# First mixer: its convolution begins during the projections, its channel norm is summed part by part, and the first loads stand in the order of their use

## The reference, cut to what matters

```
u = x @ conv_w_in                                  # 1024 -> 768 (a) + 768 (gate) + 256 (q_mem)
h = a * sigmoid(gate)
h = depthwise_conv(h, dw_w, 31 taps) + dw_b        # each channel by itself, over the tokens, causal
h = layer_norm(h, ln_g, ln_b)                      # over the 768 channels of a token
y_mix = silu(h)
y_mem = softmax(q_mem k_mem^T / 8) v_mem           # 4 heads, 256 memory rows
x = layer_norm(sqrt(2) * x + concat(y_mix, y_mem) @ w_o, ln1_g, ln1_b)
```

## Time and profile before

| | |
|---|---|
| median of 3 runs | 2316.89 us (2315.36 to 2318.26) |
| the profiled execution: its own time | 2313.38 us |
| its span in the trace | 2311.6 us |
| busy: PE, DVE, ACT, POOL | 2117.9, 1109.6, 757.2, 62.6 us |
| weights read | 597.22 MB, 259 GB/s over the span |
| the first mixer | the first 188 us of the span, about |

### The profile page before, as it was taken

One profiled execution on the slowest core, in us unless ns is written; L12 is line 12 of the kernel. 1 busy time (PEld: TensorE's weight loads), 2 busy tenths in 40 slices (PEclk: granted clock), 3 DMA queues, 4 the chain that ended last, 5 costly groups with the idle time before them and its releaser, 6 DMA issues.

```text
span 2311.6 us, 30755 instructions
## 1 busy us (share of the span) xinstructions
PE 2117.9 (92%) x13056; PEld 1530.9 (66%) x13056; DVE 1109.6 (48%) x1866; ACT 757.2 (33%) x1387; POOL 62.6 (3%) x96
## 2 busy tenths in 40 slices
PE   7968999999979899999898789999999889999998
PEld 7855434433458644344343778999998778999996
DVE  5664232222256632222222566666554466666554
ACT  4743111101135411011110545543443454543442
POOL 3000000000000000000000000010000000020000
PEclk9989999999999899999999899999999899999999
DMA  9307999999974489999999423454545514454552
GB/s 315 115 37 282 427 427 428 427 428 427 425 299 177 157 368 427 427 428 427 428 428 400 157 73 125 142 198 147 180 176 178 182 46 142 153 194 155 183 182 74
DMA packets 129054, 600.32 MB, mean 260 GB/s; under 512 B 5980, under 2 KB 24544, under 8 KB 102672
## 3 DMA queue, kind: packets, MB, share of 16 engines
q1 hardware_dynamic: 124336, 589.32, 64.4%
q10 hardware_dynamic: 3344, 7.79, 0.9%
q0 software_dynamic: 1232, 1.19, 0.3%
HBM read 597.22 MB, written 1.05 MB: 259 GB/s over the span
## 4 chain that ended last, share of the span: by engine, by line
PE 71%; DMA 16%; DVE 8%; ACT 3%; issue 1%; SPq 0%; DVEq 0%; ACTq 0%
PE ps L1458 13%; PE ps L440 10%; PE ps L441 9%; PE ps L442 9%; DMA ring<-in_w_up 8%; DMA rx<-in_w_up 8%; PE ps L1498 6%; PE ps L456 2%; PE ps L458 2%; PE ps L457 2%; DVE ARm L980 2%; PE ps L539 2%; PE ps L2835 2%; PE ps L2837 2%; PE ps L2836 2%; PE ps L1387 1%
## 5 line engine op out<-in xcount | busy, mean ns | idle before, releaser
L416 DVE TENSOR_TENSOR CL<-ring,CH 128x1024 fp32r<-128x1024 f32 x284 | 333.5, 1213 | 248.2 <-ACT CH L411 247.7
L440 PE MATMUL ps<-XTH,CH 128*128 128x256 f32 x1456 | 422.3, 290 | 14.2 <-DVE CL L416 14.2
L441 PE MATMUL ps<-XTL,CH 128*128 128x256 f32 x1456 | 416.1, 286 | 0.0
L442 PE MATMUL ps<-XTH,CL 128*128 128x256 f32 x1456 | 416.0, 286 | 0.0
L1458 PE MATMUL ps<-ring,ARM 128*64 128x512 f32 x1024 | 353.9, 611 | 30.4 <-DMA ring<-in_w_up 20.4
L1458 PE MATMUL ps<-rx,ARM 128*64 128x512 f32 x1024 | 353.7, 608 | 20.8 <-DMA rx<-in_w_up 12.7
L411 ACT ACTIVATE CH<-ring 128x1024 fp32r<-128x1024 f32 x284 | 283.2, 1044 | 122.4 <-PE ps L2837 60.7
L440 PEld LDWEIGHTS ps<-XTH,CH 128*128 128x128 f32 x1456 | 283.7, 195 | 18.2 <-DVE CL L416 15.3
L441 PEld LDWEIGHTS ps<-XTL,CH 128*128 128x128 f32 x1456 | 283.8, 195 | 0.4
L442 PEld LDWEIGHTS ps<-XTH,CL 128*128 128x128 f32 x1456 | 283.5, 195 | 0.0
L1458 PEld LDWEIGHTS ps<-ring,ARM 128*64 128x64 f32 x1024 | 114.8, 141 | 186.3 <-issue 137.6
(11 more groups left out here) (421 smaller groups left out, 3697.5 us busy)
## 6 DMA issues: line engine op xcount, KB each, us to landing
rx<-in_w_gate SPq DMA_DIRECT2D x32, 2048.0 KB, 23.6
ring<-in_w_gate SPq DMA_DIRECT2D x32, 2048.0 KB, 24.9
ring<-in_w_down SPq DMA_DIRECT2D x32, 2048.0 KB, 27.2
ring<-in_w_ffn SPq DMA_DIRECT2D x30, 2048.0 KB, 8.2
ring<-in_w_up SPq DMA_DIRECT2D x28, 2048.0 KB, 27.0
rx<-in_w_down SPq DMA_DIRECT2D x28, 2048.0 KB, 27.2
rx<-in_w_up SPq DMA_DIRECT2D x28, 2048.0 KB, 27.3
ring<-in_w_in SPq DMA_DIRECT2D x14, 2048.0 KB, 8.6
```

The source lines that it names most:

```text
L416: v.e.tensor_tensor(pc.lo[:, cs], pc.ap[:, cs], pc.hi[:, cs].bitcast(F), ALU.subtract).then_inc(dve_done, v.put("lo", pc.k, q))
L440: p.e.matmul(o, pc.hi[:, c, n0:n0 + 128], src[0][:, c, :], start=c == 0, stop=False)
L441: p.e.matmul(o, pc.hi[:, c, n0:n0 + 128], src[1][:, c, :], start=False, stop=False)
L442: m = p.e.matmul(o, pc.lo[:, c, n0:n0 + 128], src[0][:, c, :], start=False, stop=c == nk - 1)
```

## The change

1. Loads. `mem` comes in two halves; `x` moves from ACT's queue into SP's, behind `w_mem_kv`; the norm's gain and bias (`load_gb`) are issued behind the projections; 20 small loads for the router and later stages (`g_route_loads`) leave the start of POOL's queue and wait for projection u0. The weights of the convolution are loaded and cut so that pieces come in the order memory queries, a and gate of blocks 0 and 1, of 2 and 3, of 4 and 5.
2. Projections in the order `U_ORDER`, with the memory scores, exp and normalization among them. DVE multiplies `a` straight out of PSUM (no copies `CA`), and runs 20 taps between the splits.
3. Taps: 80 on TensorE (18 of j = 3, all of j = 4 and 5, block after block), 106 on DVE, those of two or three blocks in turn, most with `own(1)` in place of `own()`.
4. Norm: a first mean `M0` over blocks 0 and 1 is subtracted from each block as it gets ready; its sum and its squares are added up block by block (`SUMS`), and the variance is the mean square less the square of the mean. The end is done for each half of the tokens apart, and ACT applies SiLU twice, once for the product itself and once for its high half.
5. Output tiles: chunks 6 and 7 (the memory part) of the first four tiles are done first and left open in PSUM. `dve_router` moves behind tile (1, 1), its sums behind (2, 1).

```diff
@@ sp_all, loads
-            y.e.dma_start(MEM, I["mem"][0].rearrange("(t p) d -> p t d", p=128)).then_inc(mem_in, 16)
...
+        def y_first_loads(k):
+            if k == 0:
+                for t in range(2):
+                    y.e.dma_start(MEM[:, t, :], I["mem"][0, 128 * t:128 * t + 128, :]).then_inc(mem_in[t], 16)
+            if k == 1:
+                y.e.dma_start(X, I["x"][0].rearrange("(t p) d -> p t d", p=128)).then_inc(x_in, 16)
...
+        def g_route_loads():
+            g.wait_ge(pe_done, p.at("u", 0))
@@ taps
-        ON_PE = 9
-        taps = [(k, j) for k in range(31) for j in ((3, 4, 5, 2) if k < ON_PE else (3, 4, 5))]
+        U_ORDER = (12, 13, 0, 1, 6, 7, 2, 3, 8, 9, 4, 5, 10, 11)
+        ON_PE = 18
+        pe_taps = [(k, 3) for k in range(ON_PE)] + [(k, j) for j in (4, 5) for k in range(31)]
+        taps_a = [(k, j) for k in range(10) for j in (0, 1)]
+        taps_b = [(k, j) for i in range(21) for k, j in ((10 + i, 0), (10 + i, 1), (i, 2))]
+        taps_c = [x for i in range(31 - ON_PE) for x in ((21 + i, 2), (ON_PE + i, 3)) if x[0] < 31]
+        SUMS = (0, 1, 4, 2, 3, 5)
@@ pe_conv
+            for s, n in enumerate(U_ORDER):
+                pc = p_piece("mix0", 2 + s // 2)
+                p_feat(("u", n), pc, (s % 2) * 128, MIX[0][1], bank=4 + s % 4)
+                if s in (2, 3):
+                    p.wait_ge(act_done, a.at("u", 10 + s))
+                    p_scores(conv_jobs[s - 2])
...
+                if (k, j) == (12, 5):
+                    o = take(("first mean",), 4)
+                    p.wait_ge(dve_done, v.at("conv", 1))
...
+            for n, j in enumerate(SUMS):
+                p.wait_ge(dve_done, v.at("c", j))
+                p.e.matmul(o1[:, 0:256], C("ones"), HC[:, j, :], start=n == 0, stop=n == 5).then_inc(pe_done, p.put("sum"))
+                p.wait_ge(act_done, a.at("c", j))
+                p.e.matmul(o2[:, 0:256], C("ones"), SQ[:, n % 2, :], start=n == 0,
+                           stop=n == 5).then_inc(pe_done, p.put("squares", j))
@@ act_conv
+                if s == 4:
+                    for job in conv_jobs:
+                        a_exp(job)
@@ dve_conv
+                    v.own(0 if (k, j) in taps_c and k > 30 - (2 * (31 - ON_PE) - len(taps_c)) else 1)
+                    v.e.scalar_tensor_tensor(HC[:, j, :], HP[:, j, k:k + 256], w, HC[:, j, :], ALU.mult,
+                                             ALU.add).then_inc(dve_done, v.put())
...
+                if s in (6, 7):
+                    v_normed(conv_jobs[s - 6])
+                if s == 8:
+                    dve_lam(0)
+                if s > 5:
                     v.own()
+                    for i in range(1 if s < 8 else 3):
+                        tap(*next(begun))
...
+            for t in range(2):
+                ts = slice(128 * t, 128 * t + 128)
+                v.e.tensor_tensor(HC[:, :, ts], HC[:, :, ts], bc_mid(MEAN[:, ts], 6), ALU.subtract).then_inc(dve_done, v.put())
+                v.wait_ge(act_done, a.at("conv sd"))
+                v.e.reciprocal(RS[:, ts], SD[:, ts]).then_inc(dve_done, v.put())
@@ pe_out, dve_out
+            begun = WO_ORDER[0:4] if l == 0 else []
+            for i, (n, t) in enumerate(begun):
+                p_toks((f"wo{l}", n, t), p_piece(f"mix{l}", W_O[l] + n), t, ys, [6, 7], lambda c: ("y0", c),
+                       bank=(2, 3, 6, 7)[i], last=False)
...
+                if l == 0 and (n, t) == (1, 1):
+                    dve_router()
```

More of the change, by code:

```diff
@@ L444, in p_feat, with p_toks @@
             p.name("piece", pc.k)
-        def p_toks(key, pc, t, src, cs=range(8), ready=None, bank=None, between=None):
-            o = take(key, bank)[:, 0:256]
+        def p_toks(key, pc, t, src, cs=range(8), ready=None, bank=None, between=None, first=True, last=True):
+            o = (take(key, bank) if first else tile(*key))[:, 0:256]
             for c in cs:
@@ new lines, in pe_conv @@
+            for n, (k, j) in enumerate(pe_taps):
+                if k == 0:
+                    b = take(("conv", j), 2 + j)
+                if (k, j) == (12, 5):
+                    o = take(("first mean",), 4)
+                    p.wait_ge(dve_done, v.at("conv", 1))
+                    for i in range(2):
+                        m = p.e.matmul(o[:, 0:256], C("ones"), HC[:, i, :], start=i == 0, stop=i == 1)
+                    m.then_inc(pe_done, p.put("first mean"))
+                if (k, j) == (16, 5):
+                    for i in conv_jobs:
+                        p_turned(i)
+                if (k, j) == (29, 5):
+                    for i in conv_jobs:
+                        p_head_out(0)(i)
+                p.wait_ge(dve_done, v.at("hp", j))
@@ L888, in pe_conv @@
-            p.wait_ge(dve_done, v.at("conv", 2))
-            p.wait_ge(act_done, a.at("conv", 5))
-            for j in range(6):
-                m = p.e.matmul(b[:, 0:256], C("ones"), HC[:, j, :], start=j == 0, stop=j == 5)
-            m.then_inc(pe_done, p.put("mean"))
-            p.wait_ge(dve_done, v.at("router parts"))
-            p.e.matmul(take(("router",), 1)[:, 0:144], C("ones"), RB.rearrange("p l k n -> p (l k n)"), start=True,
-                       stop=True).then_inc(pe_done, p.put("router"))
@@ L935, in act_conv @@
-            for j in range(3, 6):
-                a.wait_ge(pe_done, p.at("conv", j))
-                a.e.activation(HC[:, j, :], tile("conv", j)[:, 0:256], ACT.Identity,
-                               bias=VT[:, j:j + 1]).then_inc(act_done, a.put("conv", j))
-            a.wait_ge(dve_done, v.at("centred"))
-            a.e.activation(SQ, HC, ACT.Square).then_inc(act_done, a.put("squares"))
-            for j in conv_jobs:
-                a_turned(j)
-            a.wait_ge(dve_done, v.at("square"))
@@ new lines, in act_conv @@
+                if 8 <= s < 12:
+                    diag(2 * s - 16)
+                    diag(2 * s - 15)
+            a_next("mix0", 9)
+            load_gb(I["ln1_g"][0], I["ln1_b"][0])
+            for n in range(8, len(pe_taps)):
+                if pe_taps[n] == (24, 5):
+                    for j in conv_jobs:
+                        a_turned(j)
+                diag(n)
+            a_warm(ACT.Sqrt)
+            for n, j in enumerate(SUMS):
+                a.wait_ge(dve_done, v.at("c", j))
+                if n > 1:
+                    a.wait_ge(pe_done, p.at("squares", SUMS[n - 2]))
+                a.e.activation(SQ[:, n % 2, :], HC[:, j, :], ACT.Square).then_inc(act_done, a.put("c", j))
@@ L1003, in dve_conv @@
+            v.wait_ge(pe_done, p.at("squares"))
             v.own()
-            v.e.reciprocal(MU, SD).then_inc(dve_done, v.put())
-            v.own()
-            v.e.tensor_tensor(HC, HC, bc_mid(MU, 6), ALU.mult).then_inc(dve_done, v.put("conv normed"))
-            for j in range(6):
-                hi, lo = y_part(0, j)
-                v.wait_ge(act_done, a.at("conv out", j))
-                v_halves(hi, lo, SQ[:, j, :]).then_inc(dve_done, v.put("y0", j))
+            v.e.scalar_tensor_tensor(SD, tile("squares")[:, 0:256], 1.0 / 768, SD, ALU.mult,
+                                     ALU.subtract).then_inc(dve_done, v.put("conv var"))
@@ L1013, in program, with centred @@
+        def centred(j, x, ready):
+            v.wait_ge(pe_done, ready)
+            v.e.scalar_tensor_tensor(HC[:, j, :], x, VT[:, j:j + 1], M0, ALU.add, ALU.subtract).then_inc(dve_done, v.put("c", j))
         MQ = mix_area(1, 3584, 1536).rearrange("p (j t) -> p j t", j=6)
```

267 lines of the change are left out of this document (145 added, 122 removed).

## The result

| | before | changed |
|---|---|---|
| median of the runs on one chip, us | 2316.12 (2314.34 to 2318.26, 4 runs) | 2297.28 (2295.79 to 2298.98, 4 runs) |
| ratio, 95% interval | | 0.9918 (0.9901 to 0.9936) |
| span of the profiled execution, us | 2311.6 | 2295.3 |
| DVE's last add into X (end of the mixer), us | 187.94 | 168.99 |

The changed kernel is 18.8 us faster. The forecast was 2293, with a range of 2284 to 2305. The mechanism that I gave is the one that runs, but for one stage: behind the projections I had DVE as the engine that ends last, and it is TensorE. The gain at the last tile is 19.0 us where I had summed 24.

The account below looks back on a forecast made before the run. TensorE was taken to bound the projections, DVE the taps, a DVE-ACT-TensorE chain the norm, with DMA-bound experts following one for one. The steps put the last tile at 163.8 instead of 187.94, 24 us sooner: 2293, range 2284 to 2305.

Parts of the forecast that it names:

- Start: Loads ahead of the first key matmul: `w_mem_kv` lands at 11.9, 3.5 us sooner (bounds 0 and 4.5); projections begin at 30.5.
- Projections: TensorE's 14 projections, 40.3 us, with memory scores, 3.6, and a wait of 1, end at 75.4.
- a sign of failure: DVE's `lam` products: the forecast fails if DVE waits more than 2 us for `CS`; 0 to 2 expected.
- A tap on DVE: DVE's taps: with `own(1)` a tap takes 0.40 us instead of 0.52; last block centred at 120.8.
- Taps on TensorE: 80 taps of 0.425 us, 34.0 in all, end at 118, 3 us ahead of DVE, which stays the bound.
- Sums and norm: Behind the last centred block: 2.2 us to the variance, SiLU starts at 125.3, last y0 at 136.4, 26.1 us sooner.
- SiLU: ACT, end of the norm: two runs of 12 instructions of 128x128 at 0.30 to 0.32 us, 3.7 us each.
- Output tiles: Behind the last y0: TensorE waits 5.1 us, (3,0) starts at 149.4, slow clock costs 2.2, last tile at 163.8.
- Passed on: Experts behind the mixer: their weight stream is tied to TensorE's first expert matmul, so the mixer's gain passes one for one.
- Taps keep 0.52: Rival on DVE's taps: the pipe drains either way, 9.6 us less, a gain of 14, 2303 us; chance 0.12.
- Projections overfill: Rival on the projections' stage: DVE's nearly full list and late `lam` loads cost 4 to 8 us, 2299; chance 0.15.
- Slower: Rival on the `lam` loads: late for good, they stall DVE and TensorE; landing at 92 gives 2321; chance 0.04.

Follow-up runs that it names:

- early taps behind: Changed kernel with the 20 taps that DVE makes among the projections moved behind the last projection; 2306.56 us, ratio 0.9956.
- norm of both halves first: Changed kernel with DVE's norm of the second half of the tokens moved ahead of the first half's low halves; 2294.96 us, ratio 0.9901.
- lam later: Changed kernel with DVE's lam products two projections later; 2297.85 us, ratio 0.9917.
- SiLU once: Changed kernel with each SiLU made once on ACT and its high half copied by DVE; 2292.76 us, ratio 0.9894.

## Why the prediction was right, by its steps

- **Start.** Landing forecast at 11.9, measured 12.56; put back to the old order, the loads cost 3.2 at the landing and 3.3 at the last tile. Right, 0.7 us too good. The projections began at 31.28 instead of the 30.5 forecast (34.00 before).
- **Projections.** TensorE's taps forecast from 75.9, first long row at 77.19: 1.3 later, 0.8 of it there when the projections began. `CS` made DVE wait 2.59 us, over the 2 that I had named as a sign of failure; only 0.6 to 0.8 of it reached the first mean. Its rows were late because they took 5.9 to 7.3 us to land and not 5.3, and were issued up to 58.7 and not 57; the 20 loads ahead of them, from which that rival started, were not the cause.
- **A tap on DVE.** 0.40 forecast, 0.397 measured; with the wait 0.52. The two pairs of the earlier trace rows had the right answer. The Trainium skill, "VectorE: DVE Perf Modes", section "The DRAIN you can't avoid", says that leaving out semaphores saves nothing, from a measurement on a row of copies; it also says, in its first paragraph, that a next op that is not held starts earlier. The rival was built on the first of these alone. For taps of 128x256 the two runs with and without the wait disagree with the first by 0.12 us a tap and 13.6 us in all, and agree with the second: a tap's record is 0.47 to 0.48 us long, and without the wait the next one starts 0.397 us behind it.
- **Taps on TensorE.** Forecast to end at 118, "3 us ahead of DVE, so DVE stays the bound". They ended at 120.4. The wait for the first mean was the 3 us forecast; the late start makes 1.3 of the 2.4, and most of the rest is a tap that took 26.61 / 61 = 0.436 us and not 0.425. "DVE stays the bound" was wrong: the twelve small products stand behind the taps, so TensorE would have ended behind DVE even at 118.
- **Sums and norm.** This is the term that was mis-sized. I took 2.2 us behind 120.8 for "square, last matmul, two small products, the variance", as if the sums of the other blocks were done by then. In TensorE's list all twelve small products (0.43 each, 5.2 us) stand behind the last tap. DVE's scaling of the sum starts at 125.33 and the variance is there at 126.75, 5.9 behind 120.85. SiLU starts at 128.97, 3.7 later than forecast.
- **SiLU.** Twelve of 128x128 were priced at 0.30 to 0.32 by ACT's diagonals; those have a scale for each partition, SiLU a scale and a bias, and took 0.386. Both runs together, and the last half of y0 is ready at 141.57 instead of 136.4: 3.7 and 1.5 of the 5.2 are these two terms.
- **Output tiles.** From the last y0 to the last tile 27.4 were forecast and 27.4 measured. Within it (3, 0) started 0.8 later than forecast (13.8 behind y0 instead of 13.0, with a wait of 4.14 and not 5.1), and the rest took 13.6 instead of 14.4, since the slow clock cost 1.0 and not 2.2. That the sum agrees is luck: two errors cancel, and in other kernels with the same wait the rest took up to 14.5.
- **Passed on.** About one for one, over 14 kernels.

So 24 became 19 mostly by one order misread on TensorE and one duration borrowed from another form of ACTIVATE. The rival "Taps keep 0.52" fell by experiment. "Projections overfill" holds in that DVE is behind from 65 to 107, with a loss of 0.7 to 1.7 us (by the run with the early taps behind) instead of 4 to 8; "Slower" didn't occur, the rows landed at most 7.3 us after their issue.

Undone one by one, the parts cost 13.6 (waits of the taps), 9.3 (early taps) and 4.1 us (loads). They sum to more than the 18.8 gained. What was added against them is measured too: 4 us of TensorE's pause and products at the first mean, 4.0 of the second SiLU up to the last y0 (2.5 at the last tile), 2.75 of the order of the two halves, 5.3 of the router's place. What splitting the norm in halves, taking the sums in parts, doing chunks 6 and 7 first or multiplying straight out of PSUM brought by itself was not run alone.

What stays open is in which executions the clock falls behind a pause of 2.4 to 3.1 us.

## What to carry to other kernels

When a tuned stage is bound by one engine in turns with another, read for both the whole list behind the last dependent instruction, not only when the data is ready: a wait in the middle of TensorE's list, with small products at its end, decided here 4 us. A wait for one's own predecessor on a chain of independent accumulations is worth a look first; it was the largest single part, and one line. And where a change moves side work (here the router), put it where the engine behind it has its data already, since a pause of TensorE can be paid twice, in the wait and, in some executions, in the clock.

## What was unexpected of the hardware

- The same pause of TensorE, 3.06 us at the same product, left the clock at 1.00 in one execution (changed kernel, 106 to 108) and was followed by 0.50 in another (norm of both halves first, 108 to 110); a pause of 2.42 was followed by 0.50 from 106 to 108 in the kernel with lam later. Of the five profiles with a pause of 3.06 or 3.07 there, three kept the clock (S - T 48.14 or 48.15) and two, norm of both halves first and SiLU once, did not. Each fall cost 1.5 to 1.7 us of S - T.
- SiLUs of 128x128 with a scale and a bias for each partition, with no wait between them, start 0.386 us apart, while each has a record of 0.48: they overlap. Those of 128x256 before have records of 0.60 and took 0.63 us each, since each waited for the one before it. So half the columns make a record of 80% of the length; what two whole ones without a wait would take was not run.
- The experts' stage, bound by DMA, shifts by itself: from the last tile (X) to the issue of layer 1's output weights 502.6 to 506.1 us passed in the 14 profiles, with no relation to the edits. Two single profiles can't tell 3 us apart there (before and changed: 503.0 and 505.4).
